# A hybrid encoder block on one core: the low decay operands of the state-space rounds are made by ScalarE instead of GpSimd

## The chip, the cores and the metric

One core of a Trainium2 chip runs the whole kernel in one launch. The metric is the device time of an execution in microseconds (us); the time of a kernel is the median of its runs. Everything is in float32, and every large matrix product is made of three products of rounded parts (high by high, high by low, low by high), so the kernel keeps a high and a low part of each operand.

## The reference

One encoder layer on two request groups (256 and 512 tokens, with 16 meta tokens in front): half a SwiGLU block, a mixer with two branches (a bidirectional Mamba-2 SSD branch and a bidirectional HGRN2 branch), half a SwiGLU block, a final norm. The change lies in the SSD branch. There the decay matrix of a chunk of 128 positions and a head is the exponential of a difference of running sums:

```python
acs = jnp.cumsum((dt * A).reshape(b, c, Q, G, Hg), axis=2)
seg = acs[:, :, :, None] - acs[:, :, None, :]
Lm = jnp.exp(jnp.where(mask, seg, -jnp.inf))
CB = jnp.einsum('bctgn,bcsgn->bctsg', Cc, Bc)
y_diag = jnp.einsum('bctsg,bctsgh,bcsghp->bctghp', CB, Lm, xdt)
```

## The kernel before

The kernel never forms the running sums. For a chunk c, a direction d and four heads it scales a 128x128 triangle of ones (`incl`) by dt*A of each head, which gives a 128x512 operand, and multiplies the strict triangle (`strict`) with it on TensorE; the product is `seg` of the four heads. As dt*A is split in a high and a low part, there are two such operands: `rh` (from `gah`, line 1919, VectorE) and `rl` (from `gal`, line 2290, GpSimd). TensorE adds both products in one PSUM bank (line 776), ScalarE takes the exponential (line 1265, tile `e`), VectorE multiplies it with the masked product of B and C (line 1939), and TensorE multiplies that with the weighted input `xdt` (line 790), which GpSimd makes (line 2298).

The heads come in four groups. A group has 12 units (6 chunks by 2 directions), worked off in four steps of three units (`S_STEPS`: step k does units 3k to 3k+2); behind the segment products of a step TensorE makes the output products of chunks that are ready (`outs`: none, one chunk, two, one, and a fifth step with two). `rh`, `rl` and the PSUM banks are rings of three, so a step's operands may be written when the products of the step before are done (semaphore `seg_mm`).

A loop (`Fori` over g, three trips) works the steps of group g beside the projections of group g+1: on TensorE each step follows one dense job of 48 matmul pairs (line 508). On the other engines, for step k:

- ScalarE: split the next weight in its high part (`ssd_split`, line 971), SiLU of the convolution before (`convolved`, line 1234), copy the job's result out of PSUM (`ssd_read`, lines 1249 to 1251), exponentials (`ssd_step`, line 1265). Exp and SiLU lie in different table sets, so each step has two table loads.
- VectorE: `rh` of the step (`decays`, line 1919), the weight's low part (line 1785), the gated outputs of finished chunks (`gates`, line 1930, which waits for `y_mm`, the output products), the five-tap convolution of 802 columns (lines 1856 and 1858), the masks (`masked`, line 1939).
- GpSimd: `xdt` of the step (`steps`), then `rl` of the next step (`decays`).

Each engine works its program in the order written. The fourth group is worked behind the loop, beside gate jobs of the next phase (`J_PA`), and has no convolution; in the loop's tail TensorE transposes the new group's inputs, updates the states (line 738) and makes the carried part (lines 750 and 759).

Of the kernel before, what the change touches and what calls it, by code (L numbers as in the profile page):

```python
# [13 lines left out]
P = 128  # L14
# [3 lines left out]
ALU = mybir.AluOpType  # L18
ACT = mybir.ActivationFunctionType
# [7 lines left out]
HEADS, GROUPS, HPG, STATE, PD = 16, 4, 4, 128, 64  # L27
# [28 lines left out]
NC = NX // P  # L56
# [19 lines left out]
def lin(s, n=0, i=None):  # L76

    return s if i is None else i * n + s
# [40 lines left out]
def build(nc, x_prompt, x_sample, meta_tokens, ffn1_norm, ffn1_w_gate_up, ffn1_w_down, mix_norm, w_in,  # L119
# [3 lines left out]
    with ctx:  # L123
        def sb(name, shape, dt=F32, where=ctx):
            return where.enter_context(nc.sbuf_tensor(name, shape, dt))

        def sem(name):
            return ctx.enter_context(nc.semaphore(name))
# [12 lines left out]
        incl = [sb(f"incl{d}", [P, P]) for d in range(2)]  # L141
# [39 lines left out]
        def ffn_mem(new, t):  # L181
# [26 lines left out]
            rl=[new(f"rl{u}", [P, HPG, P], F32R) for u in range(3)],  # L208
# [78 lines left out]
        gat_ok, xw_ok, up_mm, up_ok = sem("gat_ok"), sem("xw_ok"), sem("up_mm"), sem("up_ok")  # L287
# [3 lines left out]
        rh_ok, rl_ok, seg_mm, exp_ok = sem("rh_ok"), sem("rl_ok"), sem("seg_mm"), sem("exp_ok")  # L291
# [21 lines left out]
        S_UNITS = [(c, d) for c in range(NC) for d in range(2)]  # L313
        S_STEPS = [((0, 1, 2), ()), ((3, 4, 5), (0,)), ((6, 7, 8), (1, 2)), ((9, 10, 11), (3,)), ((), (4, 5))]
        Y_STEP = [1, 2, 2, 3, 4, 4]

        def wait(eng, sem_, n, v, G):

            if G[1] is not None or v + n * G[0] > 0:
                eng.wait_ge(sem_, lin(v + n * G[0], n, G[1]))  # L320
# [63 lines left out]
        def _(sp):  # L384
# [10 lines left out]
            for n, (src, r, k, _) in enumerate(X_TILES):  # L395
                sp.dma_start(f0["x"][n][0:k, :], src[r:r + k, :]).then_inc(x_in[n], 16)
                if n in (2, 4):
                    load(FFNS[0][3][:, D_FF * (n // 2 - 1):D_FF * (n // 2 - 1) + P], KT, n // 2 - 1)
# [87 lines left out]
        def _(pe):  # L486
# [167 lines left out]
            for n, (_, _, k, t) in enumerate(X_TILES):  # L654
                pe.wait_ge(dg_ok, n + 1)
                mm = pe.matmul(aux2[0][:, PC + t:PC + t + k], ones[0:k, :], f0["dg"][0:k, n, 0:k], start=True, stop=True)
# [306 lines left out]
        def _(act):  # L963
            own = Tally(act, act_step)

            def split(s, n=0, i=None, k=KT):

                act.wait_ge(raw_in[s % 2], lin(16 * (s // 2 + 1), 8 * n, i))
                if s >= 2 or i is not None:
                    act.wait_ge(dense_done, lin(s - 1, n, i))  # L970
                act.activation(whi[s % 2][:, 0:k, :], raw[s % 2][:, 0:k, :], ACT.Copy).then_inc(w_hi, 1)  # L971

            def read_out(s, n=0, i=None, dst=None, func=ACT.Copy, c0=0):
                act.wait_ge(dense_done, lin(s + 1, n, i))
                act.activation(dst, slot[s % 2][:, PC + c0:], func).then_inc(slot_free[s % 2], 1)
# [256 lines left out]
            def convolved(c, G):  # L1232
                wait(act, conv_ok, 4, c + 1, G)
                act.activation(m_s["co"][c][:, :], m_s["ca"][:, :], ACT.Silu, bias=m_s["gw"][:, TAPS, c:c + 1]).then_inc(co_ok, 1)

            def ssd_split(c, G):
                split(J_SSD + 6 * G[0] + c + 1, 6, G[1])

            def ssd_read(c, G):
                s = J_SSD + 6 * G[0] + c  # L1240
                if c >= 4:
                    wait(act, yz_ok, 2 * NC, 0, G)
                    read_out(s, 6, G[1], zs[c - 4], ACT.Silu, N_META)
                    return
                wait(act, conv_ok, 4, c - 1, G)
                act.wait_ge(z_ok, 2)
                act.wait_ge(dense_done, lin(s + 1, 6, G[1]))
                b, p = m_s["ci"][c % 2], slot[s % 2][:, PC:]
                own.add(act.activation(b[:, 2:2 + SPLIT], p[:, 0:SPLIT], ACT.Copy))
                own.add(act.activation(b[:, 4 + SPLIT:4 + SPLIT + N_META], p[:, 0:N_META], ACT.Copy))  # L1250
                act.activation(b[:, 4 + SPLIT + N_META:4 + SPLIT + N_META + N_S], p[:, SPLIT:], ACT.Copy).then_inc(slot_free[s % 2], 1)

            def ssd_turn(G):
                for n in range(NC + 2):
                    k = N_META if n < 2 else P
                    if n >= 2:
                        wait(act, xdt_ok, 2 * NC, 2 * (n - 1) - 2 * NC, G)
                    wait(act, tr_mm, NC + 2, n + 1, G)
                    act.activation(m_s["xbt"][0:k, n, :], aux[n % 2][0:k, 0:3 * P], ACT.Copy).then_inc(tr_ok, 1)

            def ssd_step(k, G):
                for u in S_STEPS[k][0]:
                    wait(act, seg_mm, 2 * NC, u + 1, G)
                    wait(act, y_mm, 4, Y_STEP[(u - 4) // 2] if u >= 4 else 0, G)
                    act.activation(m_s["e"][u % 4][:, :, :], aux[u % 3].rearrange("p (h t) -> p h t", h=HPG), ACT.Exp).then_inc(exp_ok, 1)
# [18 lines left out]
            with act.Fori(0, GROUPS - 1) as g:  # L1284
                G, N = (0, g), (1, g)
                for k in range(4):
                    ssd_split(k, N)
                    if k:
                        convolved(k - 1, N)
                    ssd_read(k, N)  # L1290
                    ssd_step(k, G)
                ssd_turn(N)
                ssd_split(4, N)
                convolved(3, N)
                ssd_read(4, N)
                ssd_split(5, N)
                ssd_read(5, N)
# [7 lines left out]
            last = (GROUPS - 1, None)  # L1305


            def pa_gate(t):

                if t == 3:  # L1310
                    act.wait_ge(off_mm, NC * GROUPS)
                if t == KT - 1:
                    act.wait_ge(ya_ok, KT)
                read_out(J_PA + t, dst=m_a["ga"][:, t, :], func=ACT.Sigmoid, c0=N_META)

            for k in range(5):
                split(J_PA + 1 + k)
                pa_gate(k)
                ssd_step(k, last)
            split(J_PA + 6)  # L1320
# [881 lines left out]
        def _(pool):  # L2202
# [71 lines left out]
            def ssd_weighted(G):  # L2274

                wait(pool, gat_ok, 2, 2, G)
                wait(pool, up_mm, len(S_UPD) // 2, 0, G)
                for n, (d, c) in enumerate(S_UPD):
                    q, k, m = (c - META, N_META, META) if c >= META else (c + 2, P, c)

                    wait(pool, tr_ok, NC + 2, NC + 2 if n >= 4 else q + 1, G)
                    pool.tensor_tensor(h4(xws[n][0:k, :]), h4(m_s["xbt"][0:k, q, 0:2 * P]),
                                       m_s["gw_t"][0:k, m, d, :].unsqueeze(2).broadcast_to([k, HPG, PD]), ALU.mult).then_inc(xw_ok, 1)

            def decays(k, G):
                for u in S_STEPS[k][0]:
                    c, d = S_UNITS[u]
                    wait(pool, gat_ok, 2, 2, G)
                    wait(pool, seg_mm, 2 * NC, max(u - 2, 0), G)
                    pool.tensor_tensor(m_s["rl"][u % 3][:, :, :], incl[d][:, :].unsqueeze(1).broadcast_to([P, HPG, P]),  # L2290
                                       m_s["gal"][:, c, d, :].unsqueeze(2).broadcast_to([P, HPG, P]), ALU.mult).then_inc(rl_ok, 1)

            def steps(k, G):

                for u in S_STEPS[k][0]:
                    c, d = S_UNITS[u]
                    wait(pool, y_mm, 4, Y_STEP[c - 2] if c >= 2 else 0, G)
                    pool.tensor_tensor(h4(m_s["xdt"][c % 2][d][:, :]), h4(m_s["xbt"][:, c + 2, 0:2 * P]),
                                       m_s["gdt"][:, c, d, :].unsqueeze(2).broadcast_to([P, HPG, PD]), ALU.mult).then_inc(xdt_ok, 1)

            ssd_weighted((0, None))
            with pool.Fori(0, GROUPS - 1) as g:
                G, N = (0, g), (1, g)
                decays(0, G)
                for k in range(4):
                    steps(k, G)
                    if k < 3:
                        decays(k + 1, G)
                ssd_weighted(N)
            last = (GROUPS - 1, None)  # L2310
            for k in range(4):
                decays(k, last)
                steps(k, last)
            for t in range(6, KT + 1):
                low(J_PA + t)
# [74 lines left out]
```

## Time and profile before

| what | value |
|---|---|
| median of 3 runs | 2397.02 us (2396.19 to 2397.97) |
| the profiled execution | 2390.29 us, its span 2388.8 us |
| TensorE busy | 2274.7 us, 95% of the span |
| VectorE, ScalarE, GpSimd busy | 1464.7, 977.7, 471.0 us |
| chain that ended last | TensorE 73%, VectorE 12%, "issue" 7%, ScalarE 5% |

A profile is one execution, with times in us from the start of the span. PE is TensorE's matmul, PEld its weight load, DVE VectorE, ACT ScalarE, POOL GpSimd. A row names a line of the kernel, an operation and its tiles (out<-in). Matmuls overlap, so differences of starts say more than their durations.

### The profile page before, as it was taken

Reading aid. Unit: us, or ns where it says so; the run is one execution under the profiler, and the core shown is the slowest. Engines: PE = TensorE matmul, PEld = TensorE weight load, DVE = VectorE, ACT = ScalarE, POOL = GpSimd, SP = SyncE. Lnnn points to the kernel's source line nnn. Section 1 sums busy time; section 2 is a strip of 40 time slices with the busy share of each in tenths; the row PEclk is TensorE's granted clock in tenths of the full one; section 3 lists DMA queues with packets and bytes.
Section 4 is the critical chain, followed back from the end, with each engine's and each line's share of the span. In section 5 each row is a group of like instructions: output and inputs, shape, how many; then the busy total and the mean of one; then the engine's idle time right before and its main releaser. Section 6 shows DMA issues by size and latency. Waiting matters only on the chain.

```text
span 2388.8 us, 36367 instructions
## 1 busy us (share of the span) xinstructions
PE 2274.7 (95%) x13195; PEld 2027.8 (85%) x13195; DVE 1464.7 (61%) x2324; ACT 977.7 (41%) x1475; POOL 471.0 (20%) x336
## 2 busy tenths in 40 slices
PE   7899999998989998999999999999999899999997
PEld 6799999997877786888888888888888799999996
DVE  5777676678778888632444454442233777676677
ACT  6333242344433523432566566544124343242343
POOL 2300000000033333233333333322333300000000
PEclk8899999998999999999999999999999999999999
DMA  3122222213111111123211111111332122231211
GB/s 112 51 71 58 67 83 57 71 36 124 45 36 27 35 35 32 48 66 102 54 45 44 44 36 43 36 45 45 101 128 64 51 71 66 59 88 53 71 53 71
DMA packets 252272, 144.64 MB, mean 61 GB/s; under 512 B 5712, under 2 KB 248576, under 8 KB 252176
## 3 DMA queue, kind: packets, MB, share of 16 engines
q1 hardware_dynamic: 249072, 130.63, 19.6%
q0 software_dynamic: 2336, 12.58, 1.5%
q8 instruction: 62, 1.02, 0.2%
q14 instruction: 34, 0.28, 0.0%
q10 hardware_dynamic: 768, 0.13, 0.0%
HBM read 133.89 MB, written 9.44 MB: 60 GB/s over the span
## 4 chain that ended last, share of the span: by engine, by line
PE 73%; DVE 12%; issue 7%; ACT 5%; POOL 1%; DMA 1%; ACTq 0%; DVEq 0%; POOLq 0%
PE slot L508 26%; PE aux L539 23%; PE slot L587 13%; DVE ca L1858 2%; PE aux L899 1%; PE aux L790 1%; PE aux L776 1%; PE aux L867 1%; POOL wlo L2208 1%; PE aux L892 1%; PE aux L880 1%; DVE e L1939 1%; ACT whi L971 1%; PE slot L666 1%; PE aux L786 1%
## 5 line engine op out<-in xcount | busy, mean ns | idle before, releaser
L2208 POOL TENSOR_TENSOR wlo<-raw,whi 128x1024 fp32r<-128x1024 f32 (+1 forms) x100 | 223.8, 2238 | 1045.2 <-ACT whi L971 1045.2
L508 PE MATMUL slot<-xh,whi 128*128 128x256 f32 (+1 forms) x1360 | 361.6, 347 | 8.6 <-POOL wlo L2208 6.5
L508 PE MATMUL slot<-xh,wlo 128*128 128x256 f32 (+1 forms) x1360 | 351.6, 340 | 0.0
L508 PE MATMUL slot<-xl,whi 128*128 128x256 f32 (+1 forms) x1360 | 350.5, 340 | 0.0
L508 PEld LDWEIGHTS slot<-xh,whi 128*128 128x128 f32 x1360 | 252.7, 188 | 46.8 <-POOL wlo L2208 8.4
L508 PEld LDWEIGHTS slot<-xl,whi 128*128 128x128 f32 x1360 | 256.1, 189 | 29.9
L508 PEld LDWEIGHTS slot<-xh,wlo 128*128 128x128 f32 x1360 | 255.8, 188 | 30.1
L539 PE MATMUL aux<-th,whi 128*128 128x392 f32 (+1 forms) x640 | 221.7, 346 | 4.6 <-ACT work L1077 4.6
L1051 ACT ACTIVATE whi<-work 128x512 fp32r<-128x512 f32 x220 | 135.7, 626 | 209.3 <-DVE work L1589 112.1
L539 PE MATMUL aux<-tl,whi 128*128 128x392 f32 (+1 forms) x640 | 218.1, 341 | 0.0
L539 PE MATMUL aux<-th,wlo 128*128 128x392 f32 (+1 forms) x640 | 216.6, 338 | 0.0
L1568 DVE TENSOR_TENSOR wlo<-work,whi 128x512 fp32r<-128x512 f32 x220 | 151.4, 689 | 85.3 <-ACT whi L1051 85.3
L539 PE MATMUL aux<-xh,whi 128*128 128x392 f32 (+1 forms) x480 | 164.5, 343 | 9.9 <-DVE wlo L1568 7.4
L539 PE MATMUL aux<-xl,whi 128*128 128x392 f32 (+1 forms) x480 | 163.8, 341 | 0.0
L539 PE MATMUL aux<-xh,wlo 128*128 128x392 f32 (+1 forms) x480 | 163.5, 341 | 0.0
L971 ACT ACTIVATE whi<-raw 128x1024 fp32r<-128x1024 f32 (+1 forms) x129 | 125.4, 972 | 87.5 <-PE slot L508 73.2
L587 PE MATMUL slot<-ah,whi 128*128 128x272 f32 (+1 forms) x608 | 159.0, 343 | 1.4 <-DVE al L1610 0.8
L587 PE MATMUL slot<-ah,wlo 128*128 128x272 f32 (+1 forms) x608 | 156.9, 339 | 0.0
L587 PE MATMUL slot<-al,whi 128*128 128x272 f32 (+1 forms) x608 | 156.9, 339 | 0.0
L1656 DVE SCALAR_TENSOR_TENSOR gate<-slot,rs 128x784 f32<-128x784 f32 (+1 forms) x76 | 73.4, 966 | 102.1 <-PE slot L587 102.0
L539 PEld LDWEIGHTS aux<-th,whi 128*128 128x128 f32 x640 | 120.9, 189 | 14.5 <-issue 10.2
L587 PEld LDWEIGHTS slot<-ah,whi 128*128 128x128 f32 x608 | 113.4, 188 | 16.9 <-issue 3.4
(333 smaller groups left out, 4451.6 us busy)
## 6 DMA issues: line engine op xcount, KB each, us to landing
raw<-in_w_in SPq DMA_DIRECT2D x81, 512.0 KB, 3.9
raw<-in_ffn_w_gate_up SPq DMA_DIRECT2D x48, 512.0 KB, 4.2
work<-in_ffn_w_gate_up SPq DMA_DIRECT2D x40, 512.0 KB, 4.8
raw<-in_ffn_w_down SPq DMA_DIRECT2D x80, 256.0 KB, 3.1
raw<-in_ssd_w_proj SPq DMA_DIRECT2D x8, 512.0 KB, 4.1
raw<-in_hg_w_proj SPq DMA_DIRECT2D x8, 512.0 KB, 3.9
raw<-in_w_out SPq DMA_DIRECT2D x8, 512.0 KB, 3.9
h_spill<-h POOLq DMA_DIRECT2D x1, 3072.0 KB, 10.9
```

Of the source, the lines that this page charges most:

```text
L508: mm = pe.matmul(slot[b][:, PC + u:PC + v], w[b][:, t, :], x[:, t, u + off:v + off], start=(t == 0 and p == 0 and q == 0), stop=(t == k - ...
L539: mm = pe.matmul(aux[bank][:, 0:NT - mid], w[:, t, :], x, start=(first and t == 0 and n == 0), stop=(t == HK - 1 and n == 2), skip_group_c ...
L587: mm = pe.matmul(slot[d % 2][:, PC + u:PC + e], quarter(w, v)[:, t, :], x[:, t, u:e], start=(t == 0 and n == 0), stop=(t == PAIRS - 1 and ...
L666: return pe.matmul(slot[j % 2][:, PC + u:PC + v], w[j % 2][:, t, :], x[:, t, u:v], start=first, stop=last)
L776: mm = pe.matmul(aux[u % 3][:, :], strict[d][:, :], v[u % 3][:, :, :], start=(p == 0), stop=(p == 1))
L786: pe.matmul(aux[3][:, h:h + P], yoff[:, c, P * q:P * (q + 1)], ident[:, :], start=True, stop=False, skip_group_check=True)
L971: act.activation(whi[s % 2][:, 0:k, :], raw[s % 2][:, 0:k, :], ACT.Copy).then_inc(w_hi, 1)
L1051: act.activation(quarter(whi, v), operand(m_, n % 2), ACT.Copy).then_inc(q_hi, 1)
L1568: dve.tensor_tensor(quarter(wlo, v), operand(m_, n % 2), quarter(whi, v).bitcast(F32), sub).then_inc(q_lo, 1)
L1656: dve.scalar_tensor_tensor(m["t"][:, c0:], slot[b][:, PC + c0:], 0.5, rs[:, c0:], mul, mul).then_inc(dn_free[b], 1)
L1858: ins = dve.scalar_tensor_tensor(ca[:, :], ci[:, k:k + CO], m_s["gw"][:, k, c:c + 1], ca[:, :], ALU.mult, ALU.add)
L2208: pool.tensor_tensor(wlo[s % 2][:, 0:k, :], raw[s % 2][:, 0:k, :], whi[s % 2][:, 0:k, :].bitcast(F32), ALU.subtract).then_inc(w_lo, 1)
```

## The change

GpSimd's `decays` is deleted, with its calls. ScalarE gets a `decays` that writes the same `rl` tiles under the same waits, but one head at a time: an activation Copy of the 128x128 triangle with the head's column of `gal` as its scale, four for each unit, twelve for each step. In each step it stands behind the split of the weight.

```diff
+            def decays(k, G):
+                for u in S_STEPS[k][0]:
+                    c, d = S_UNITS[u]
+                    wait(act, gat_ok, 2, 2, G)
+                    wait(act, seg_mm, 2 * NC, max(u - 2, 0), G)
+                    for h in range(HPG):
+                        ins = act.activation(m_s["rl"][u % 3][:, h, :], incl[d][:, :], ACT.Copy, scale=m_s["gal"][:, c, d, h:h + 1])
+                    ins.then_inc(rl_ok, 1)
@@ ScalarE, loop over groups, and behind it
                 for k in range(4):
                     ssd_split(k, N)
+                    decays(k, G)
                     if k:
                         convolved(k - 1, N)
...
             for k in range(5):
                 split(J_PA + 1 + k)
+                decays(k, last)
                 pa_gate(k)
@@ GpSimd
-            def decays(k, G):
-                for u in S_STEPS[k][0]:
-                    c, d = S_UNITS[u]
-                    wait(pool, gat_ok, 2, 2, G)
-                    wait(pool, seg_mm, 2 * NC, max(u - 2, 0), G)
-                    pool.tensor_tensor(m_s["rl"][u % 3][:, :, :], incl[d][:, :].unsqueeze(1).broadcast_to([P, HPG, P]),
-                                       m_s["gal"][:, c, d, :].unsqueeze(2).broadcast_to([P, HPG, P]), ALU.mult).then_inc(rl_ok, 1)
...
-                decays(0, G)
                 for k in range(4):
                     steps(k, G)
-                    if k < 3:
-                        decays(k + 1, G)
...
             for k in range(4):
-                decays(k, last)
                 steps(k, last)
```

## Rows read from the trace of the kernel before

**Rows 1.** The first loop trip: busy time and instructions by engine, PEclk, DMA share, GB/s
```profile
685.57:779.39 93.82, 86.30 (x509) 69.60 (x508) 78.62 (x115) 35.02 (x52) 34.04 (x34) 0.98 0.13 34
```
**Rows 2.** TensorE's waits in the three trips: total us, times, longest us
```profile
PE aux L776 <- DVE rh L1919: 12.8, 9, 2.4
PE aux L759 <- DVE prev L1894: 6.5, 3, 2.2
```
**Rows 3.** TensorE in order of time, steps 1 to 3: start us, us, instruction, idle before
```profile
696.12 0.50 PE L776 MATMUL aux<-rh,strict 128*128 128x512 f32 x1 [0.42 <-DVE rh L1919]
...
699.22 0.66 PE L790 MATMUL aux<-e,xdt 128*64 128x128 f32 x8
...
710.09 0.50 PE L776 MATMUL aux<-rh,strict 128*128 128x512 f32 x1 [1.45 <-DVE rh L1919]
...
715.22 0.66 PE L790 MATMUL aux<-e,xdt 128*64 128x128 f32 x8
...
727.05 0.50 PE L776 MATMUL aux<-rh,strict 128*128 128x512 f32 x1 [2.40 <-DVE rh L1919]
...
728.83 0.38 PE L786 MATMUL aux<-ident,prev 128*128 128x128 f32 x2
```
**Rows 4.** TensorE in order of time, step 2 of the last group
```profile
988.62 0.39 PE L776 MATMUL aux<-rh,strict 128*128 128x512 f32 x1
...
990.01 0.38 PE L786 MATMUL aux<-ident,prev 128*128 128x128 f32 x2
```
**Rows 5.** VectorE in order of time, steps 0 and 1 of the first trip
```profile
687.79 5.87 DVE L1858 SCALAR_TENSOR_TENSOR ca<-ci,gw,ca 128x802 f32<-128x802 f32 x4
...
701.10 6.53 DVE L1858 SCALAR_TENSOR_TENSOR ca<-ci,gw,ca 128x802 f32<-128x802 f32 x4
707.56 1.88 DVE L1939 TENSOR_TENSOR e<-e,prev 128x512 f32<-128x512 f32 x3
```
**Rows 6.** Line 1858 alone in convolutions of steps 2 and 3: DVE busy, PEclk, DMA, GB/s
```profile
716.74:724.10 7.36, 6.36 (x4) 1.00 0.02 3
733.62:738.60 4.98, 4.21 (x4) 1.00 0.00 0
```
**Rows 7.** GpSimd in order of time, steps 1 and 2
```profile
699.99 1.55 POOL L2298 TENSOR_TENSOR xdt<-xbt,gdt 128x256 f32<-128x256 f32 x2 [8.27 <-PE aux L790]
701.50 5.29 POOL L2290 TENSOR_TENSOR rl<-incl,gal 128x512 fp32r<-128x512 f32 x3
715.98 2.09 POOL L2298 TENSOR_TENSOR xdt<-xbt,gdt 128x256 f32<-128x256 f32 x3 [9.20 <-PE aux L790]
```
**Rows 8.** ScalarE in order of time: copies with a column as their scale
```profile
16.50 3.41 ACT L1005 ACTIVATE xh<-h,vec_b 128x272 fp32r<-128x272 f32 x8 [2.07 <-DVE vec_b L1748]
...
27.05 1.33 ACT L1005 ACTIVATE xh<-h,vec_b 128x512 fp32r<-128x512 f32 x2 [1.62 <-DVE h L1735]
```
**Rows 9.** ScalarE in order of time, first trip, and the last group's second gate
```profile
689.49 1.07 ACT L971 ACTIVATE whi<-raw 128x1024 fp32r<-128x1024 f32 x1
...
693.69 0.97 ACT L1234 ACTIVATE co<-ca,gw 128x802 f32<-128x802 f32 x1 [1.83 <-DVE ca L1858]
695.74 0.40 ACT L1249 ACTIVATE ci<-slot 128x272 f32<-128x272 f32 x1 [1.08 <-PE slot L508]
...
696.72 1.28 ACT L1265 ACT_TABLE_LOAD   x1
698.01 0.60 ACT L1265 ACTIVATE e<-aux 128x512 f32<-128x512 f32 x1
...
707.67 0.97 ACT L1234 ACTIVATE co<-ca,gw 128x802 f32<-128x802 f32 x1 [4.39 <-DVE ca L1858]
...
736.04 1.05 ACT L971 ACTIVATE whi<-raw 128x1024 fp32r<-128x1024 f32 x1
...
976.97 0.81 ACT L975 ACTIVATE ga<-slot 128x768 f32<-128x768 f32 x1 [3.87 <-PE slot L508]
```
**Rows 10.** All engines from step 3 of the second trip: columns as in rows 1
```profile
820.80:826.00 5.20, 5.12 (x27) 3.50 (x28) 2.37 (x4) 0.94 (x2) 0.00 (x0) 0.67 0.23 58
```

## The prediction

> **What bounds the kernel now.** I read the totals first: TensorE is busy 95% of the span and GpSimd, which loses work, 20%, so the `rl` operations as such are worth nothing. Then I looked only at the stretch in which they run. Each trip of the loop takes 93.8 us, of which TensorE is busy 86.3 [rows 1]; the three trips are alike within 0.1 us. The waits of TensorE in these trips name `rh`, made by VectorE, 12.8 us in nine waits, and `prev` of the carried part, 6.5 us in three [rows 2]. Nobody waits for `rl`. In order of time the waits for `rh` are 0.42, 1.45 and 2.40 us, ahead of steps 1, 2 and 3 [rows 3], and the pattern repeats in every trip. A late step costs a bit more: its three units then follow VectorE's pace, 1.78 us to the next instruction (727.05 to 728.83), where an undelayed step needs 1.39 [rows 3, 4], so 0.39 more.
>
> Why is VectorE late? Its order is convolution, masks, `rh`. The convolution of step 3, with GpSimd idle, takes 4.98 us; that of step 2, with `rl` and `xdt` on GpSimd throughout, 7.36 us [rows 6]. DMA share is 0.02 and 0.00 in the two, so DMA is not the difference. In step 1 `rl` begins at 701.50, just after line 1858's first instruction at 701.10, and the four take 6.46 us to the masks at 707.56, in step 0 5.87 [rows 5, 7]; alone they would take about 4.3 (4.98 less the first tap). The same `rl` whose time is free on its own engine slows the engine on which TensorE waits.
>
> **The change, part by part.**
>
> *Removed from GpSimd:* 48 operations, twelve a group. In step 1 three of them take 5.29 us [rows 7]. `xdt` stays: three, contended, take 2.09 us, 0.70 each [rows 7]. The loss of VectorE per us of overlap is (7.36 - 4.98) / 7.36 = 0.32 us [rows 6].
>
> *Added to ScalarE:* twelve activations a step, 192 in all. The trace has no 128-column copy with a column scale, but line 1005 is the same form: eight of 272 columns in 3.41 us and two of 512 in 1.33 [rows 8]; with an overlap of 0.1 us between neighbours that is 0.41 and 0.615 us each, a slope of 0.84 ns per column, so 0.29 us for 128 columns and 3.6 us for twelve. Bounds: no less than the fixed part, 0.19 us (2.3 us a step), no more than the 272-column row, 0.41 us (5.1 us a step). I take 3.6, nearest to the rows.
>
> Queued behind these are the SiLU, the PSUM copy, and the exponentials; who waits for them is VectorE's convolution and masks, then TensorE. Step 0: the copies stand in a long idle stretch of ScalarE ahead of the job's end and cost nothing. Step 1: split from 689.49 to 690.56, `rl` ready at 694.15 (TensorE wants it at 695.70), table load, SiLU from 695.4 to 696.3 instead of 693.69 to 694.7, so the PSUM copy starts at 696.3 instead of 695.74 [rows 9], 0.6 us late. The exponentials that follow still wait for `y_mm` at 699.1, and the next convolution starts only after the gates at 699.2: hidden. Steps 2 and 3: ScalarE idles 4.39 us before SiLU in step 2 and as much in step 3 [rows 9], and 3.6 us fit; convolutions that end 2 us sooner use the rest, but then the PSUM copy waits for TensorE anyway. Last group: there the table load, not the SiLU, precedes the gate; the idle time before the gate is 3.87 us [rows 9], so 3.6 fits, barely, and nobody waits for that gate soon. At the bound of 5.1 us a step `rl` of step 1 is ready at 695.66, still just in time. So this part costs 0; with the cover gone, see the third rival.
>
> Do ScalarE's copies slow VectorE as GpSimd did? The split at 736.04, SBUF to SBUF, lies inside the undisturbed convolution of step 3 [rows 6, 9]. I take 0.
>
> *Sum, in the first trip's times.* Step 1: the convolution of step 0 saves up to 1.6 us against a wait of 0.42, so TensorE starts at 695.70. Its outputs ended 3.76 us after its start (696.12 to 699.22 + 0.66 = 699.88); less the 0.39 of a late step that is 3.37, so 699.07. Step 2: TensorE's own side is the job, 8.76 us (699.88 to 710.09, less 1.45), so 707.83. VectorE's side is 1.22 us to line 1858 (699.88 to 701.10), 4.3 + 0.15 for what two `xdt` overlap, and 2.53 for masks and first `rh` (707.56 to 710.09), so 707.3: in time. TensorE starts at 707.83, and its outputs end 5.79 - 0.39 us later (710.09 to 715.88), at 713.23. Step 3: the job brings TensorE to 722.0 (715.88 to 727.05 less 2.40 is 8.77). VectorE's side is 0.86 us to the convolution (715.88 to 716.74), 4.98 for it plus 0.68 for 2.1 us of overlap (now four `xdt` of 0.70 us run back to back, as nothing stands between the third and fourth), and 2.53, so 722.3. The wait shrinks from 2.40 to 0.3. A trip gains 727.05 - 722.3 = 4.75 us, three trips 14.2 us. The wait for `prev` [rows 2] hangs on TensorE's own state products of the same trip and stays, and the last group has no waits to remove. Gain 14.2 us: 2390.3 to 2376.1 for the profiled execution. The median shown is 6.7 us above it, so I forecast 2382.8, say 2383. With the step-3 overlap at twice the loss the gain is 12; with all three waits gone it is 16.
>
> *A rule against this change.* ScalarE's table load occupies 1.28 us, from 696.72, and the exponential starts at 698.01, 1.29 us after it [rows 9]. The Trainium skill ("ScalarE: Activation LUTs", What ACT_TABLE_LOAD costs) counts about 2.66 us for each switch, with a drain. By that price, an estimate, ScalarE would have two switches of 2.66 in each step beside the copies, the last exponentials of a trip would come 2 us late, and the gain would be about 8 us, 2389. The row shows the next activation without that drain, so I keep 14.2.
>
> **Rivals.**
>
> 1. *VectorE isn't freed.* The convolutions stay slow, because `xdt`, or ScalarE's copies now lying beside them, disturb as much as `rl` did. For it: nothing here shows twelve small activations beside a convolution. Against it: the split at 736.04. Gain 0 to 3 us, 2394 to 2397. Chance 0.09.
>
> 2. *The clock takes or gives.* In each trip TensorE's granted clock falls once after an idle stretch; in the second trip this follows the 2.40 us wait, and 5.2 us then run at 0.67 of full clock, part of it at 1.2 GHz [rows 10], a loss of 1.7 us. With the long wait gone a trip may lose this fall or get another elsewhere. Each trip has 0.98 now [rows 1], and trips with the fall in other places are no shorter, so I expect no change. One fall more a trip: gain 9 us, 2388. One less: 19 us, 2378. Chance 0.13 together.
>
> 3. *ScalarE becomes the bound (slower).* Place: `rl` of steps 1 to 3. From the end of the split TensorE leaves 5.1 us in step 1 (690.56 to 695.70) and by the same counting about 6.6 and 6.1 in steps 2 and 3. Twelve activations of c us exceed the old waits' sum of 4.3 us a trip, and the last group's similar slack, from c = 0.57 us on. At 0.75 us the loops would lose some 15 us and the last group 10: 2422. Against it: 0.57 us is more than a copy of 272 columns [rows 8]. A milder form of it is a late SiLU in step 1 that delays the exponentials; it would cost 0.6 us a trip. Chance 0.05.
>
> 4. *Half of it.* Some wait behind the removed one takes part: `rh` of step 3 at 0.3 us is already next, step 2 has only 0.5 us to spare, and transposes and exponentials follow. Gain 5 to 10 us, 2387 to 2392. Chance 0.11.
>
> **How the numbers follow.** The forecast has 0.62, with its own range 2380 to 2386. The remaining cases are added to it until 8 in 10 are held: 2378 to 2390. A difference under 0.2% (4.8 us) can't be told from none here. Faster by more: forecast, both clock cases and rival 4, together 0.86. Within: rival 1, 0.09. Slower: 0.05.
>
> **What would show it.** The three waits for `rh` at 0, 0 and 0.3 us; convolutions of steps 0 to 2 near 5.0, 5.1 and 5.7 us; trips of 89 us; ScalarE's scaled copies near 0.39 us each in duration and 0.29 from start to start; no wait of TensorE for `rl`; the last group's 52 us unchanged. It is wrong if the convolutions stay over 6.5 us, if TensorE waits for an activation of line `decays`, or if trips shorten by less than 2 us.

## The result, and the profile after

The changed kernel takes 2374.96 us (median of 6 runs, 2373.63 to 2378.13), the kernel before 2395.68 us (6 runs, 2391.02 to 2397.97); the ratio is 0.9917, with a 95% interval of 0.9907 to 0.9927, so about 20 us faster. (One of the 52 executions of before that were taken beside all these kernels took 3168.77 us at a mean granted clock of 0.653; it is left out of every median and ratio here.) I forecast 2383 us and 2378 to 2390: the sign was right, the time lies 3 us outside the range. The profiled execution took 2374.89 us with a span of 2373.4 us, 15.4 us below the span of before.

The three trips, columns as in [rows 1], where each took 93.8 us:
```profile
685.66:774.56 88.90, 85.40 (x509) 69.78 (x508) 74.35 (x115) 48.91 (x100) 15.62 (x22) 0.98 0.13 36
774.56:863.53 88.97, 85.48 (x509) 69.84 (x508) 74.21 (x115) 48.91 (x100) 15.63 (x22) 0.98 0.13 35
863.53:950.82 87.29, 83.79 (x510) 68.49 (x509) 74.08 (x112) 50.18 (x101) 15.62 (x22) 1.00 0.14 36
```
They are 4.9, 4.8 and 6.5 us shorter. Of the busy times, counted from TensorE's, ScalarE's (the fourth) is 14 us longer a trip and GpSimd's (the fifth) 18 us shorter; VectorE's (the third) is 4 us shorter with the same instructions. The third trip is 1.6 us shorter than the others, and it alone has the full clock (PEclk, the granted share of TensorE's full clock, is 1.00).

TensorE's waits in these trips, as in [rows 2]:
```profile
PE aux L759 <- DVE prev L1906: 6.5, 3, 2.2
PE aux L723 <- ACT xbt L1259: 2.2, 9, 0.3
PE aux L723 <- ACT e L1275: 1.0, 3, 0.3
PE aux L776 <- DVE rh L1931: 0.7, 3, 0.2
```
The nine waits for `rh`, 12.8 us, are three of 0.7 us together; the wait for `prev` is what it was. Nothing waits for `rl`.

TensorE in order of time, at the places of [rows 3]: step 1, 2 and 3, and the instruction behind step 3's products:
```profile
695.62 0.40 PE L776 MATMUL aux<-rh,strict 128*128 128x512 f32 x1
...
707.62 0.40 PE L776 MATMUL aux<-rh,strict 128*128 128x512 f32 x1
...
722.04 0.53 PE L776 MATMUL aux<-rh,strict 128*128 128x512 f32 x1 [0.24 <-DVE rh L1931]
...
723.82 0.38 PE L786 MATMUL aux<-ident,prev 128*128 128x128 f32 x2
```
VectorE beside them, against [rows 5] (line 1870 is line 1858 of before):
```profile
687.53 4.33 DVE L1870 SCALAR_TENSOR_TENSOR ca<-ci,gw,ca 128x802 f32<-128x802 f32 x4
...
700.22 4.55 DVE L1870 SCALAR_TENSOR_TENSOR ca<-ci,gw,ca 128x802 f32<-128x802 f32 x4
...
714.79 4.79 DVE L1870 SCALAR_TENSOR_TENSOR ca<-ci,gw,ca 128x802 f32<-128x802 f32 x4
```
ScalarE, against [rows 9]: twelve scaled copies end at 694.15, and the PSUM copy that stood at 695.74 stands at 696.33:
```profile
690.53 3.62 ACT L1268 ACTIVATE rl<-incl,gal 128x128 fp32r<-128x128 f32 x12
694.16 1.28 ACT L1234 ACT_TABLE_LOAD   x1
695.46 0.97 ACT L1234 ACTIVATE co<-ca,gw 128x802 f32<-128x802 f32 x1
696.33 0.38 ACT L1249 ACTIVATE ci<-slot 128x272 f32<-128x272 f32 x1
```
GpSimd, against [rows 7]; the fourth `xdt` now follows at once:
```profile
699.10 1.55 POOL L2302 TENSOR_TENSOR xdt<-xbt,gdt 128x256 f32<-128x256 f32 x2 [40.27 <-PE aux L790]
713.13 3.42 POOL L2302 TENSOR_TENSOR xdt<-xbt,gdt 128x256 f32<-128x256 f32 x4 [12.48 <-PE aux L790]
```

### The profile page after: what moved, and what is told of

Read it like the earlier page. It is cut to its first block, busy times and chain, and to the rows that moved or that the text cites. A ratio compares the mean times of both kernels' runs of the same rounds, so it can differ in the third digit from the quotient of the medians.

```text
span 2373.4 us, 36511 instructions
## 1 busy us (share of the span) xinstructions
PE 2270.0 (96%) x13195; PEld 2025.9 (85%) x13195; DVE 1446.3 (61%) x2324; ACT 1033.2 (44%) x1667; POOL 401.5 (17%) x288
## 4 chain that ended last, share of the span: by engine, by line
PE 76%; DVE 10%; issue 7%; ACT 5%; POOL 1%; DMA 0%; ACTq 0%; DVEq 0%; POOLq 0%
PE slot L508 29%; PE aux L539 23%; PE slot L587 13%; PE aux L899 1%; PE aux L790 1%; PE aux L776 1%; PE aux L867 1%; POOL wlo L2220 1%; PE aux L892 1%; PE aux L880 1%; PE aux L759 1%; ACT whi L971 1%; PE slot L666 1%; PE aux L786 1%; DVE ca L1870 1%
```

## Experiments

Two questions. Does the gain come from VectorE's freedom, as I said, or from something that ScalarE or the earlier `rl` does? And why do the runs differ by 20 us where the sum said 14 and the profiles 15?

**no_low_operand**: `rl` left out altogether.

```diff
-                    wait(pe, rl_ok, 2 * NC, u + 1, G)
-                    for p, v in enumerate((m_s["rh"], m_s["rl"])):
+                    for p, v in enumerate((m_s["rh"], m_s["rh"])):
```
(and `decays` of `rl` with its calls, and VectorE's wait for it, deleted: neither ScalarE nor GpSimd makes `rl`, and the kernel leaves out the low part of the decays)

> The kernel before with the low operand left out: nobody makes rl, and TensorE's second segment product reads rh again (same count and shape of matmuls; the decays lose their low part). Main theory: the gain is VectorE's freedom from GpSimd's rl and nothing else, and ScalarE's 192 copies cost nothing; so this equals the changed kernel within 1.5 us (ratio 0.991 to 0.993), trips near 88.9 us, convolutions 5.0, 5.2 and 5.6 us. Rival (ScalarE's copies have a hidden price): this is 3 us or more faster than the changed kernel.

Measured: 2375.4 us, ratio 0.9912 (0.9896 to 0.9928), where the changed kernel beside it had 0.9909. Trips of 88.8, 88.8 and 88.9 us. VectorE's convolutions:
```profile
687.24 4.33 DVE L1857 SCALAR_TENSOR_TENSOR ca<-ci,gw,ca 128x802 f32<-128x802 f32 x4
...
699.93 4.55 DVE L1857 SCALAR_TENSOR_TENSOR ca<-ci,gw,ca 128x802 f32<-128x802 f32 x4
...
714.50 4.79 DVE L1857 SCALAR_TENSOR_TENSOR ca<-ci,gw,ca 128x802 f32<-128x802 f32 x4
```
Their durations are those of the changed kernel to the last digit, and a trip is as long as one of the changed kernel with a fall of the clock (of which more below). So ScalarE's 192 copies neither slow VectorE nor delay the path by anything that these runs can tell.

**copy_on_gpsimd**: the changed kernel, and GpSimd does its old work for nothing.

```diff
+            def decays(k, G):      # on GpSimd, called where it was before
...
+                    pool.tensor_tensor(m_s["rd"][:, :, :], incl[d][:, :].unsqueeze(1).broadcast_to([P, HPG, P]),
+                                       m_s["gal"][:, c, d, :].unsqueeze(2).broadcast_to([P, HPG, P]), ALU.mult).then_inc(rd_ok, 1)
```

> The changed kernel, ScalarE makes rl, and beside it GpSimd does its old rl operations at their old places into a tile that nobody reads. Main theory: the convolutions are 6.5 to 7.4 us again, the waits for rh come back at 0.4, 1.4 and 2.4 us, trips 93.8 us, ratio 0.998 to 1.001. Rival (what helps is that rl is ready sooner, or the shorter GpSimd program): most of the gain stays, ratio under 0.995.

Measured: 2397.3 us, ratio 1.0009 (0.9999 to 1.002). The whole gain is gone. VectorE's convolutions of steps 0 to 2, then TensorE's waits in the trips:
```profile
689.14 5.87 DVE L1872 SCALAR_TENSOR_TENSOR ca<-ci,gw,ca 128x802 f32<-128x802 f32 x4
...
702.47 6.53 DVE L1872 SCALAR_TENSOR_TENSOR ca<-ci,gw,ca 128x802 f32<-128x802 f32 x4
...
719.00 6.54 DVE L1872 SCALAR_TENSOR_TENSOR ca<-ci,gw,ca 128x802 f32<-128x802 f32 x4
```
```profile
PE aux L778 <- DVE rh L1934: 13.2, 9, 2.4
```
As before, though `rl` is ready as early as in the changed kernel. What costs is GpSimd's work beside VectorE. The trips were longer than I expected, 95.5 us each; the next runs say why.

**before_again, after_again, before_third, after_third**: both kernels unchanged, profiled again.

> The kernel before, unchanged, profiled a second time. My forecast carried over a difference of 6.7 us between the profiled execution of before (2390.3 us) and the median of its first runs (2397.0 us). Theory A (clock): executions of before differ by how often TensorE's granted clock falls after an idle stretch, so a profile that is longer than 2388.8 us has its excess in stretches with a granted clock under 0.99, and the three loop trips stay near 93.8 us each or are 1.5 us longer for each fall more. Theory B (offset): the difference is start and end of an execution and not in the span; then the span is again 2388 to 2390 us, and the time minus the span is over 5 us. Ratio to before 1.000 within 0.001 by both.

> The changed kernel, unchanged, once more. Both theories: ratio 0.991 to 0.993. The first profile had trips of 88.9, 89.0 and 87.3 us, the third without a fall of the clock. Theory A: the second profile has trips of 87.3 or 88.9 us and nothing between, by falls of the clock; time minus span is 1.5 us as before.

> The kernel before, a third profile, to count falls of TensorE's clock in the three trips. Profiles so far: 3 and 5 in six places (the waits of over 2 us), trips of 93.8 us with one fall and 95.2 with two, 92.4 with none by the filled kernel. Theory A: each trip is again one of these three lengths within 0.2 us, and 3 to 6 falls.

> The changed kernel, a third profile. So far 2 and 2 falls in three places, trips of 87.3 us with none and 88.8 with one. Theory A: each trip is again one of these two lengths within 0.2 us, 1 to 3 falls.

Measured: before_again 2396.15 us, ratio 1.0003; after_again 2374.5 us, ratio 0.9909 (0.9894 to 0.9924); before_third 2396.3 us and after_third 2373.34 us, one run each. Time less span was 1.4 to 1.6 us in every run, in the long ones too, so the excess of a long execution lies in its span (theory B is out).

The second profile of before has its three trips so:
```profile
686.41:781.50 95.09, 87.59 (x510) 70.85 (x509) 78.56 (x115) 35.02 (x52) 34.05 (x34) 0.96 0.13 34
781.50:876.72 95.22, 87.73 (x510) 70.76 (x509) 78.75 (x115) 35.02 (x52) 34.05 (x34) 0.96 0.12 33
876.72:970.50 93.78, 86.28 (x510) 69.25 (x509) 78.48 (x112) 36.31 (x53) 34.05 (x34) 0.98 0.13 34
```
Two of them are 1.4 us longer than those of [rows 1], with a granted clock of 0.96 instead of 0.98. The place, TensorE at step 3 of the first trip:
```profile
727.90 0.74 PE L776 MATMUL aux<-rh,strict 128*128 128x512 f32 x1 [2.40 <-DVE rh L1919]
728.44 0.63 PE L776 MATMUL aux<-rl,strict 128*128 128x512 f32 x1
728.87 0.63 PE L776 MATMUL aux<-rh,strict 128*128 128x512 f32 x1
```
The pitch from start to start is 0.43 us where the same matmuls at full clock have 0.23: the lower level, 1.2 GHz, right behind the idle stretch. I call this a fall of the clock.

The third profile of before has trips of 93.9, 95.0 and 95.1 us, the other two of the changed kernel 87.3, 88.7, 88.7 and 87.3, 87.3, 88.7. The lengths fall in classes: for before one fall of the clock (93.8) or two (95.0), for the changed kernel none (87.3) or one (88.7 to 88.9). In the trips the falls come behind the two waits of over 2 us alone: for `rh` of step 3 and for `prev`. Before has six such places in its trips and 3, 5 and 5 falls in three profiles (copy_on_gpsimd, with the same waits, 6); the changed kernel has three places and 2, 2 and 1 falls (no_low_operand 3).

Theory A holds for the trips, but they are only about half of it: they hold 2.7 of the 5.7 us by which the second profile of before is longer than the first, and 2.5 of the third's 6.0 us. The rest lies ahead of the loop and behind it. Part of that is low clock too (from 1618 to 1626 us the second profile has a granted clock of 0.57, the first 1.00); how much is not worked out here.

**fill_before, fill_after**: work without a use in these waits.

```diff
+                if k == 3 and G[1] is not None:           # fill_before alone
+                    wait(pe, exp_ok, 2 * NC, 7, G)
+                    for _ in range(8):
+                        pe.matmul(aux[0][:, :], xh[:, 0, 0:P], xh[:, 0, 0:BANK], start=True, stop=True)
...
+                    if c == 2 and G[1] is not None:       # both, in the carried part
...
+                        for _ in range(8):
+                            pe.matmul(slot[b][:, 0:BANK], xh[:, 0, 0:P], xh[:, 0, 0:BANK], start=True, stop=True)
```

> The kernel before; ahead of its wait for rh of step 3 and ahead of its wait for prev in the carried part, each trip, TensorE does 8 matmuls of 512 columns that nobody reads (1.9 us of work in waits of 2.4 and 2.2 us). The waits' ends don't move. Theory A (the clock falls behind these idle stretches, by chance now at one and now at the other, and this is why executions of before scatter and lie above its first profile): no fall in the trips, each 92.3 to 92.4 us, so 4 to 8 us less than before, ratio 0.997 to 0.998. Rival (the falls have nothing to do with the idle stretches): ratio 1.000, falls as before.

> The changed kernel with the same 8 matmuls ahead of its wait for prev alone. Theory A: no fall in the trips, each 87.3 us; 2 to 4 us less than the changed kernel, ratio to before 0.990 to 0.991. Rival: as the changed kernel, trips of 88.9 us with a fall each in two of three.

Measured: fill_before 2387.9 us, ratio 0.9974 (0.9962 to 0.9986); fill_after 2373.0 us, ratio 0.9906 (0.9892 to 0.9921). The trips, first those of fill_before:
```profile
685.61:778.00 92.39, 88.57 (x526) 71.18 (x525) 78.53 (x115) 35.03 (x52) 34.03 (x34) 1.00 0.13 35
778.00:870.34 92.34, 88.52 (x525) 71.16 (x524) 78.51 (x115) 35.03 (x52) 34.03 (x34) 1.00 0.13 34
870.34:962.70 92.36, 88.53 (x526) 71.16 (x525) 78.70 (x112) 36.31 (x53) 34.03 (x34) 1.00 0.13 34
```
and those of fill_after:
```profile
685.82:773.11 87.29, 85.65 (x518) 70.12 (x516) 74.16 (x115) 48.91 (x100) 15.61 (x22) 1.00 0.14 37
773.11:860.38 87.27, 85.60 (x517) 70.10 (x516) 74.15 (x115) 48.91 (x100) 15.61 (x22) 1.00 0.13 36
860.38:947.65 87.27, 85.61 (x518) 70.11 (x516) 74.28 (x112) 50.18 (x101) 15.60 (x22) 1.00 0.14 36
```
More work, and before is faster by 0.26%, clear of its interval. No fall in nine filled waits; the trips of a kernel agree within 0.05 us. fill_after's gain over the changed kernel is too small for its interval to show; its trips show it. The two fences also give the change's own price without the clock: 92.36 - 87.28 = 5.08 us a trip, 15.2 us in all. The medians of the two filled kernels differ by 14.9 us, those of the unfilled ones by 20.7 us. Each interval is some 3 us wide to either side, so the difference of the two is rough, but it points the same way: part of the gain is falls of the clock that the change removes.

**twenty_copies**: how much slack has ScalarE?

```diff
                     for h in range(HPG):
+                        if u % 3 < 2:
+                            act.activation(m_s["rd"][u % 3][:, h, :], incl[d][:, :], ACT.Copy, scale=m_s["gal"][:, c, d, h:h + 1])
```

> The changed kernel with 20 instead of 12 activations in each step on ScalarE (8 more of the same form into a tile nobody reads, for the first two units of each step): 5.95 instead of 3.6 us a step. By the slack worked out from the rows, step 1 just holds, step 2 makes rl 0.9 us late and step 3's exponentials and the transposes come 1.5 to 2 us late: 2.5 to 3 us a trip, and half a us in the last group, so 2382 to 2385 us. Rival (ScalarE has no slack): 12 steps of 2.35 us more, 2403 us. Rival (ScalarE isn't on the way at all): 2375 us.

Measured: 2381.4 us, ratio 0.994 (0.9927 to 0.9952): slower than the changed kernel by some 6 us, nearest to what the slack says and just under its range. But the profile has the trips at 88.60, 88.62 and 88.66 us without a fall: 1.35 us longer than fill_after's, half of what I expected. `rl` of step 2 is late by 0.45 us, and the first transposes wait 0.83 instead of 0.34 us for the exponentials. The span is 7.8 us longer than in the first profile of the changed kernel: 2.0 us ahead of the loop, 0.7 in the trips (that profile had two falls there) and 5.1 behind them. About 3 us of these 5.1 come with a stretch at half the clock in a later phase, columns as in [rows 1]:
```profile
1602.87:1609.69 6.82, 6.56 (x31) 6.56 (x31) 1.80 (x10) 0.00 (x0) 0.00 (x0) 0.50 0.01 2
```
before_again and fill_before have such a stretch at the same place of the program, without any of these copies, and the changed kernel's three profiles have none. Whether more copies make it more frequent is not shown, so the 6 us are not the price of eight copies a step; the 1.35 us a trip and 0.7 us in the last group are what the trace shows of that. That its waits for `prev`, still 2.17 us, had no fall in three trips shows that the fall isn't certain behind such a wait.

**late_sum, late_sum_2**: shorten the wait for `prev`.

```diff
             with dve.Fori(0, GROUPS - 1) as g:
...
-                    low(J_SSD + 6 + k + 1, 6, g)
+                    if k:                                  # late_sum_2 alone
+                        low(J_SSD + 6 + k + 1, 6, g)
...
-                weighted(G)
+                weighted(G, True)                          # without the last add and scaling
...
                 ssd_carried(N)
+                low(J_SSD + 12 + 1, 6, g)                  # late_sum_2 alone
+                weighted_end(G)
```
(late_sum_2 also makes the first such low part ahead of the loop, and leaves out the one behind the loop that would be made twice)

> The changed kernel; in the loop the second half of the norm's sum (line weighted, its last add and scaling, 1.65 us on VectorE) stands behind the carried part instead of ahead of rh of step 0. The wait for prev shrinks from 2.17 to about 0.5 us; the convolution of step 0 starts 1.2 us later against TensorE, which its slack of 1.4 us holds. 1.65 us a trip, 5 us in all, and by theory A the falls of the clock behind this wait go as well, another 2 to 4 us: trips 85.6 us, 2366 to 2370 us, ratio 0.988 to 0.989. Rival (the clock doesn't follow the wait): 2370 us, trips of 87.2 us where the clock falls.

Measured: 2376.7 us, ratio 0.9916 (0.9902 to 0.9929), no better than the changed kernel. The wait for `prev` shrank to 0.53 us and no trip had a fall, but another wait took part of the place in trips 2 and 3:
```profile
775.18 0.62 PE L508 MATMUL slot<-xh,whi 128*128 128x272 f32 x2 [1.23 <-DVE wlo L1797]
```
I had reckoned with `rh` of step 1 behind the moved work and not with the low part of job 1's weight, which VectorE makes earlier.

That wait isn't what made the run no better. The three trips (85.65, 87.1 and 87.1 us) are together 4.5 us shorter than those of the changed kernel in the mean of its three profiles (259.9 against 264.4 us). The profile lost this again behind the loop, which took 6.1 us longer than in the first profile of the changed kernel; 4.9 us of it come with three falls of the clock in the next phase:
```profile
1359.70:1363.10 3.40, 3.40 (x19) 3.40 (x18) 0.72 (x5) 0.00 (x0) 0.00 (x0) 0.50 0.00 0
1424.50:1428.00 3.50, 3.50 (x19) 3.50 (x19) 0.82 (x5) 0.00 (x0) 0.00 (x0) 0.51 0.00 0
1489.40:1492.90 3.50, 3.50 (x19) 3.50 (x19) 0.79 (x5) 0.00 (x0) 0.00 (x0) 0.51 0.00 0
```
The edit doesn't touch that phase, and the longest wait of TensorE just ahead of each is 0.58 us; the changed kernel has the same wait there and no fall. Of the five executions two took 2372.1 and 2372.4 us and three 2376.7 to 2378.3, a distance of about these three falls.

> The changed kernel with the late half of the norm's sum, but now VectorE makes the low part of the weight of job 1 (1.1 us, line 1785 of before) ahead of that half and not behind it: in the run late_sum TensorE waited 1.23 us for that low part in two of three trips. Theory: no such wait, wait for prev 0.53 us, step 1's rh just in time; each trip 85.6 us without a fall of the clock (it was 85.65 in the first trip of late_sum), so 5 us less than the changed kernel without falls and up to 3 more for the falls: 2366 to 2370 us, ratio 0.988 to 0.990. Rival: the late half makes rh of step 1 late as well, by 1 us or more a trip; then it is no better than the changed kernel.

Measured: 2367.2 us, ratio 0.9885 (0.9868 to 0.9903), the fastest of all, as forecast: trips of 85.6, 86.1 and 86.1 us with no fall, 6.5 us less in all than the changed kernel's in the mean. Its interval lies clear of that of the changed kernel. Of the 9.5 us to late_sum only 2.0 lie in the trips, where the wait for `wlo` is gone; this profile has none of the three falls behind the loop.

## Why the prediction was right in its steps and wrong in its time

**VectorE as what TensorE waits for, and GpSimd's `rl` as what slows it**: right, and shown from both sides (no_low_operand, copy_on_gpsimd).

**ScalarE's price**: right. Twelve copies take 3.62 us (forecast 3.6), a copy 0.39 us; step 1's PSUM copy comes at 696.33 (forecast 696.3). The table load stands at 694.16 and the SiLU follows at 695.46, 1.30 us later. The Trainium skill ("ScalarE: Activation LUTs", What ACT_TABLE_LOAD costs) has about 2.66 us for a switch; this trace does not agree, and the measurement decides. The trip keeps its slack: with eight more copies a step it loses 1.35 us.

**The steps of the first trip**: forecast 695.70, 707.83 and 722.3, measured 695.62, 707.62 and 722.04 (the trip began 0.09 later). A trip without falls gains 5.08 us instead of 4.75. The difference is spread: step 1 starts 0.17 us earlier in the trip than forecast, from there to step 2 TensorE needs 0.13 us less, and from there to step 3 0.05 us less. The overlap with four `xdt` was sized well: the convolution of step 2 takes 5.61 us (713.89 to 719.50), so it costs 0.63 us where I counted 0.68.

**The step that failed** is the clock term, which the forecast puts at nothing: "trips with the fall in other places are no shorter, so I expect no change". The forecast is the median shown less 14.2 us, and it missed by 7.8 us. Three terms make up 6.9 of them:

- The clock, 3.8 us. The change removed three of the six places in the trips at which the clock falls. Before has 4.3 falls in an execution (mean of three profiles), the changed kernel 1.7; that is 2.7 fewer, by about 1.4 us each. fill_before shows that such a fall is due to the wait: with the waits filled no trip has one.
- The base, 2.1 us. "The median shown is 6.7 us above it" took the median of three executions. Over 51 executions of before it is 2394.95 us, not 2397.02. The rest of the 6.7 us was no offset that every kernel has: the first profile of before was a short one, with 3 falls where the next two had 5 and with less time lost outside the trips as well, and for the changed kernel the median lies 0.1 us above the profiled execution.
- The stretch itself, 1.0 us: 15.2 instead of 14.2 us.

The last 0.9 us stay open; the parts outside the trips alone differ by up to 3.5 us between the profiles of one kernel.

**The clock rival** had the mechanism. Its branch "one less" a trip, a gain of 19 us, is nearly what came: 2.7 fewer falls in three trips and a gain of 20 us; its 2378 us are 3 us off because of the base. I gave both branches together 0.13. With one profile, in which each trip happened to have exactly one fall, I took for a constant what is drawn anew in each execution.

## What to carry to other kernels

An engine whose own time is free may be what slows the one on the path: compare the same instruction in a stretch with the neighbour busy and one with it idle before costing a move at nothing. A removed wait of TensorE can be worth more than its length: here waits of 2.2 to 2.4 us were worth, in part of the executions, 1.4 us of low clock behind them as well. A profile is one draw from a spread: count from several profiles how often such an event comes before pricing it at nothing, and set the base by many runs. And when a run disappoints, look where its time went: late_sum kept its gain in the trips and lost it in a phase that the edit doesn't touch.

## What the runs showed of the hardware

Eight matmuls of no use in each wait of 2.2 to 2.4 us kept the granted clock of the trips at 1.00 (2.4 GHz) and made the kernel before 0.26% faster. Whether the clock falls behind such a wait differs between executions of one program (13 of 18 places in three profiles of before). Long waits aren't the only places: late_sum's profile has three falls behind waits of no more than 0.58 us. Line 1858's instruction takes 1.05 us alone and up to 1.72 us beside GpSimd's `rl`; beside ScalarE's copies it takes no longer than without them (four in 4.55 us in step 1 of the changed kernel and of no_low_operand).
